# Four products of the second block's mixer in seven quarter products instead of eight, with GpSimd making the weight sums; the gathers' first batches and last search moved

## The reference, cut to what matters

```
def peer_ffn(h, w_q, sub_keys, u, v):
    q = (ht @ w_q).reshape(T, PEER_HEADS, 2, PEER_DKEY // 2)
    s = jnp.einsum('thpc,hpnc->thpn', q, sub_keys)
    v1, i1 = lax.top_k(s[:, :, 0], K)
    v2, i2 = lax.top_k(s[:, :, 1], K)
    ...                      # best 16 of the 256 sums of a head: idx, and g by softmax
    a = jnp.einsum('thkd,td->thk', jnp.take(u, ib, axis=0), xb)
    return jnp.einsum('thk,thkd->td', gelu(a) * gb, jnp.take(v, ib, axis=0))

def token_mixer(h, w_in, w_conv, b_conv, b_igate, b_fgate, ...):
    xin = h @ w_in
    qa, ka, va, qm, km, vm, og, ig, fg = jnp.split(xin, cuts, axis=-1)
    attn = dilated_attention(rms(qa), rms(ka), va)
    qkm = silu(causal_short_conv(concat([qm, km]), w_conv, b_conv))     # 4 taps
    hm = mlstm_chunkwise(heads(qm), heads(km), heads(vm), log_i, log_f)
    hm = sigmoid(og) * rms_norm(hm, mlstm_norm_g)
    return concat([attn, hm]) @ w_out
```

## Time and profile before

| | us |
|---|---|
| three runs, median (range) | 1301.77 (1300.29 to 1303.67) |
| the profiled execution | 1299.79 |
| its span in the trace | 1296.4 |
| PE / DVE / ACT / POOL busy | 1189.7 / 890.4 / 251.0 / 321.2 |
| mean granted TensorE clock, share of full speed | 0.972 |

### The profile page before, as it was taken

How to read it: one execution, slowest core, us unless ns; L and a number is a source line. 1 busy time by engine, 2 the same in 40 slices (tenths; PEclk the granted TensorE clock), 3 DMA queues, 4 the chain that set the end, 5 groups by cost and what they waited for, 6 DMA issues and landing times.

```text
span 1296.4 us, 13569 instructions
## 1 busy us (share of the span) xinstructions
PE 1189.7 (92%) x4848; PEld 727.3 (56%) x4848; DVE 890.4 (69%) x2011; ACT 251.0 (19%) x644; POOL 321.2 (25%) x276
## 2 busy tenths in 40 slices
PE   8999999989998888777899887978999999999998
PEld 7657997664555444333334333333347557999943
DVE  4766865488787767777786775656448876567656
ACT  2133210221111111112211112111211441112100
POOL 0100000145554344354435544544000000000000
PEclk9999999999999999899899999889999999999999
DMA  8441657799999999999999999999657756437441
GB/s 321 169 156 66 246 209 272 282 395 396 421 421 420 422 415 419 418 417 413 415 417 418 421 388 422 421 422 421 227 215 256 215 195 250 173 112 252 183 154 64
DMA packets 92754, 399.23 MB, mean 308 GB/s; under 512 B 6480, under 2 KB 9936, under 8 KB 59792
## 3 DMA queue, kind: packets, MB, share of 16 engines
q0 software_dynamic: 37440, 270.30, 50.6%
q1 hardware_dynamic: 55248, 128.08, 27.9%
HBM read 397.30 MB, written 1.06 MB: 307 GB/s over the span
## 4 chain that ended last, share of the span: by engine, by line
PE 58%; DMA 25%; DVE 12%; ACT 2%; issue 2%; POOL 1%; SPq 0%; DVEq 0%; ACTq 0%
DMA big<-in_peer_uv,idx_t 24%; PE ps L955 12%; PE ps L1265 10%; PE ps L668 10%; PE ps L680 9%; DVE big L2259 5%; PE ps L1329 5%; PE ps L829 2%; PE ps L1193 2%; DMA wring<-in_w_in 1%; PE ps L860 1%; PE ps L728 1%; PE ps L1276 1%; ACT rows L1513 1%; POOL big L1755 1%
## 5 line engine op out<-in xcount | busy, mean ns | idle before, releaser
L955 PE MATMUL ps<-big,rows 128*128 128x512 f32 x1024 | 487.9, 633 | 96.5 <-ACT rows L1513 96.1
L955 PEld LDWEIGHTS ps<-big,rows 128*128 128x128 f32 x1024 | 202.1, 202 | 363.4 <-issue 363.4
L2259 DVE CUSTOM_DVE_ANT_0 big<-big 128x1024 f32<-128x1024 f32 x256 | 307.9, 1225 | 138.1 <-DMA big<-in_peer_uv,idx_t 135.1
L1755 POOL DMA_INDIRECT big<-in_peer_uv,idx_t x256 | 309.9, 1210 | 374.2 <-PE ps L955 312.5
L668 PE MATMUL ps<-wring,big 128*128 128x512 f32 (+1 forms) x304 | 125.9, 571 | 0.0
L1507 ACT ACTIVATE small<-small 128x4 f32<-128x4 f32 (+2 forms) x68 | 13.9, 205 | 511.3 <-DVE small L2264 501.7
L680 PE MATMUL ps<-big,wring 128*128 128x256 f32 x512 | 112.3, 379 | 0.0
L680 PEld LDWEIGHTS ps<-big,wring 128*128 128x128 f32 x512 | 96.6, 190 | 13.2 <-issue 0.5
L668 PEld LDWEIGHTS ps<-wring,big 128*128 128x128 f32 x304 | 57.0, 190 | 62.6 <-issue 61.0
L1513 ACT ACTIVATE rows<-const,small 128x128 f32<-128x128 f32 x256 | 82.2, 390 | 20.4 <-DVE small L2268 19.8
L1265 PE MATMUL ps<-big,wring 128*128 128x128 f32 x576 | 66.7, 275 | 0.9 <-DVE big L2579 0.9
(11 more groups left out here) (340 smaller groups left out, 1228.9 us busy)
## 6 DMA issues: line engine op xcount, KB each, us to landing
wring<-in_w_in SPq DMA_DIRECT2D x16, 2048.0 KB, 8.4
wring<-in_w_ada SPq DMA_DIRECT2D x8, 2048.0 KB, 7.8
wring<-in_w_gate SPq DMA_DIRECT2D x5, 2048.0 KB, 8.1
wring<-in_w_down SPq DMA_DIRECT2D x5, 2048.0 KB, 7.7
big<-in_w_ada SPq DMA_DIRECT2D x4, 2048.0 KB, 10.6
wring<-in_w_up SPq DMA_DIRECT2D x4, 2048.0 KB, 7.9
wring<-in_w_out SPq DMA_DIRECT2D x3, 2048.0 KB, 7.9
wring<-in_peer_wq SPq DMA_DIRECT2D x3, 2048.0 KB, 20.9
```

The costliest lines, as they stand in the source:

```text
L955: last = nc.tensor.matmul(banks[h], diag[:, k % DIAGS, :], v_part[:, ring_at(k), h * 512:(h + 1) * 512], start=False, stop=(k % SLOTS == S ...
L1755: pool.indirect_dma_start(pair_ring[:, ring_at(k), :], None, a["peer_uv"], bass.IndirectOffsetOnAxis(idx_t[:, k:k + 1], 0))\
L2259: nc.vector.tensor_tensor_reduce(u_part[:, ring_at(k), :], u_part[:, ring_at(k), :], h_t[:, b, :], 1.0, 0.0, ALU.mult, ALU.add, a_dot[:, i ...
```

## The change

1. The four products `in2_v`, `in2_qm`, `in2_km`, `in2_vm` are cut into quarters (two token blocks or halves of columns, two halves of the 1024 inputs) and made by seven products P1 to P7 of quarters, as in the feed-forward part. P1, P6, P7 and P4 add up in one PSUM bank ("x"), P5 and P3 in another ("z"), P2 stands alone ("y").
2. DVE makes four sums of the input once (`mix_in`). POOL makes four sums of the weight tile per product (`mix_made`: 128 x 1024 each, the fourth in place in the tile), for each of the four tiles.
3. ACT copies partial results out (`mix_copy`, 128 x 256), DVE adds three pairs per product (`mix_add`, 128 x 256). The convolutions now read their input from SBUF (`conv_in`), since it is a sum of parts.
4. PSUM banks of this stretch are given by hand (`MIX_BANKS`, `LATE_TURN`). ACT's `rsqrt(DA_STAT)` stands behind its copy of P4 of the first product.
5. Gather stage: `kept_query` is cut into 1 + 2 + 1 quarters around batches 1 and 2, `turn_query(1)` goes ahead of batch 0 on PE and `scale(1, 1, gain)` ahead of the dots of batch 0 on DVE; rows 16 to 19 go to places 1 to 4 and rows 20 and 21 to places 8 and 9; the last search starts after batch 43 instead of 42.

```diff
-    starts = {(0, 1): 2, (0, 2): 8, (0, 3): 14, (1, 0): 20, (1, 1): 26, (1, 2): 34, (1, 3): 42}
+    starts = {(0, 1): 2, (0, 2): 8, (0, 3): 14, (1, 0): 20, (1, 1): 26, (1, 2): 34, (1, 3): 43}
...
-    place = [1, 2, 3, 4, 5, 6, 7, 0] * 2 + [8, 9]
+    place = [1, 2, 3, 4, 5, 6, 7, 0] * 2 + [1, 2, 3, 4, 8, 9]
...
             query("peer_q1", 0)
+            turn_query(1)
             experts(0, banks)
-            turn_query(1)
             score(0, 1)
+            wait_turned("n2T", [1])
+            reserved("peer_q1", 1)
+            kept_query(range(0, 1))
             experts(1, banks)
-            wait_turned("n2T", [1])
+            kept_query(range(1, 3))
+            experts(2, banks)
             begin("peer_q1", 1)
-            kept_query(range(4)).then_inc(product_done, 1)
-            experts(2, banks)
+            kept_query(range(3, 4)).then_inc(product_done, 1)
...
-            by_rows("in2_v", hT2, blocks=[0])
+            mix(0, "P1")
+            mix(0, "P2")
             wait_turned("n4T", [1])
             by_rows("in2_q", hT2, blocks=[1])
             by_rows("in2_k", hT2, blocks=[1])
-            by_rows("in2_v", hT2, blocks=[1])
-            for n in ("in2_qm", "in2_km"):
-                by_cols(n, src=hT2)
+            for t, product in MIX_ORDER[2:MIX_ORDER.index((3, "P1"))]:
+                mix(t, product)
...
+            def mix_made(t):
+                q, n = [[mix_quarter(t, f, k) for k in range(2)] for f in range(2)], TILE_NO[MIX_TILES[t]]
+                add = nc.gpsimd.tensor_tensor
+                pool.wait_ge(tile_landed[n % W_SLOTS], 16 * (n // W_SLOTS + 1))
+                if t:
+                    wait_step(pool, t - 1, "P5")
+                add(mix_sums(0), q[1][0], q[1][1], ALU.add).then_inc(mix_summed, 1)
...
+                add(mix_sums(1), mix_sums(0), q[0][0], ALU.subtract).then_inc(mix_summed, 1)
...
+                add(mix_sums(2), q[0][1], mix_sums(1), ALU.subtract).then_inc(mix_summed, 1)
+                add(q[1][0], q[0][0], q[1][0], ALU.subtract).then_inc(mix_summed, 1)
...
+            for t in range(4):
+                mix_made(t)
             pool.wait_ge(ada_made, ADA_ORDER.index(9) + 1)
             gate_row(0)
...
             for m in range(HALF_BATCHES):
                 dots(m)
                 if m == 0:
-                    scale(1, 1, gain)
                     best_keys(0, 0, 1)
...
-                    wait_product(dve, n, h)
+                    if h:
+                        wait_copied(dve, i + 1, "P4")
+                        wait_added(dve, i + 1, "P7")
+                    else:
+                        wait_added(dve, i + 1, "P2")
                     for c2 in range(2):
                         ch = 4 * i + 2 * h + c2
-                        z = bank((n, h), S, c2 * S)
+                        z = conv_in[i + 1][:, (2 * h + c2) * S:(2 * h + c2 + 1) * S]
```

More of the change, by code:

```diff
@@ L206, in product_list @@
     p += half("n3T", 1) + [("ple0", 1), ("ple1", 1), ("in2_q", 0), ("in2_k", 0)] + half("n4T", 1)
[L207 to L209 removed]
+    p += [("mix_y", 0), ("in2_q", 1), ("in2_k", 1), ("mix_z", 0, 0), ("mix_x", 0, 0)]
+    for t in (1, 2):
+        p += [("mix_z", t, 0), ("mix_z", t, 1), ("mix_y", t), ("mix_x", t, 0), ("mix_x", t, 1)]
+    p += [("d_qT", b) for b in range(NB)] + [("d_kT", b) for b in range(NB)] + [("if_parts",), ("mix_y", 3), ("in2_if",)]
+    p += [("d_S", 0, i, g) for i in range(2) for g in range(2)] + [("mix_z", 3, 0), ("m_cols",), ("m_M", 0), ("m_M", 1)]
+    p += [("mix_x", 3, 0)]
     p += [("d_S", 1, i, g) for i in range(2) for g in range(2)] + [("m_S", h) for h in range(GH)] + [("in2_og", 0)]
@@ L1088, in _ @@
             last.then_inc(product_done, 1)
-            by_rows("in2_vm", hT2, blocks=[0])
+            mix(3, "P1")
+            mix(3, "P2")
+            mix(3, "P5")
             wait_moved(pe, "if_parts")
@@ L1106, in scored @@
                         last.then_inc(product_done, 1)
+            mix(3, "P6")
             scored(0)
-            by_rows("in2_vm", hT2, blocks=[1])
+            mix(3, "P3")
+            mix(3, "P7")
             pe.wait_ge(m_rows, 1)
@@ L1123, in _ @@
                 last.then_inc(product_done, 1)
+            mix(3, "P4")
             scored(1)
@@ L1134, in _ @@
             for b in range(NB):
-                wait_moved(pe, "in2_vm", b)
+                wait_added(pe, 3, "P7")
+                wait_copied(pe, 3, "P4")
                 def pair(s_b, h):
@@ L1597, in _, with mix_copy @@
             rms(3, 1)
-            move(va[:, 0, :], "in2_v", 0)
+            def mix_copy(t, product):
+                if product == "P4":
+                    wait_chain(act, t, "x")
+                    to = mix_out(t, 1, 0)
+                else:
+                    if product == "P1" and t >= 2:
+                        act.wait_ge(mix_added, 3 * (t - 1))
+                    wait_step(act, t, product)
+                    to = mix_part(t, ("P1", "P5", "P6", "P7").index(product))
+                nc.scalar.activation(to, mix_bank(t, "z" if product == "P5" else "x"), ACT.Copy).then_inc(mix_copied, 1)
+                if product == "P4":
+                    wait_copied(act, t, "P4")
+                    for n in range(1 + int(MIX_COLS[t])):
+                        act.sem_inc(emptied("mix_x", t, n), 1)
+            for t, product in MIX_COPIES[:MIX_COPIES.index((0, "P4")) + 1]:
+                mix_copy(t, product)
             rsqrt(DA_STAT)
@@ L1601, in _ @@
             exp_and_tanh()
-            move(va[:, 1, :], "in2_v", 1)
+            for t, product in MIX_COPIES[MIX_COPIES.index((0, "P4")) + 1:MIX_COPIES.index((3, "P1"))]:
+                mix_copy(t, product)
             for c in range(2):
@@ L2274, in _ @@
             out_added(1, 1)
+            scale(1, 1, gain)
             for m in range(HALF_BATCHES):
```

181 lines of the change are left out of this document (166 added, 15 removed).

## The result

The changed kernel is slower: 1318.78 us, median of four runs (1317.56 to 1320.62), against 1301.03 (1300.12 to 1303.67) for the kernel before; the ratio is 1.0133, 95% interval 1.0121 to 1.0145, so 17.7 us. Its profiled execution took 1318.88 us with a span of 1316.6. That lies in the predicted range of 1295 to 1320, near its upper end, 4.8 us above the 1314 predicted.

What follows compares the result with a forecast made beforehand. PE was taken as busiest, with DVE only 2.7 us ahead and then full in the mixer, and DMA pacing the gathers. Sum: 1299.8 - 1.5 - 2.2 + 16.2 = 1312.3 profiled, 1314 as median; 8-in-10 range 1295 to 1320.

Steps and rivals of the forecast that it cites:

- What bounds the kernel: Mixer stage: DVE 2.7 us ahead of PE at the row chain, then full, so further PE gains become waits.
- POOL's sums, the deciding term: Mixer stage: POOL's sixteen additions and DVE's SBUF instructions block each other in turns; m_rows 15.8 us late; chance 0.55.
- The wait of 8 us before the fourth product: Mixer stage: in2_vm is loaded 11 us late, so PE idles about 8 us ahead of its product.
- +16.2 at the end of the stage: End of the mixer stage: net lateness with full blocking, after 1.0 of additions less 0.6 of slack; bounds -1.9 and +16.2.
- the 12 to 17 us named as a sign: Mixer stage: being longer by this much was to show the blocking forecast right.
- PE alone 6.0 us: Mixer products: seven quarter products in place of eight save PE 3.3 us by rows and 2.7 by columns.
- the mixer 1.9 faster with no hold-up: Mixer stage: if POOL blocks nobody, 1.9 of PE's 6.0 us come through, as DVE is full.
- the rival at 1296: Mixer stage: a POOL read does not hold DVE up; 5.6 us gained in all; chance 0.25.
- The convolution from SBUF: DVE's convolutions: three taps fall from 1.52 to 1.26 us, 0.4 saved per channel, 3.2 in all, bounds 0 and 4.
- Banks cost nothing: PSUM banks: those reused first wait for DVE steps ahead of the data anyway; without that cover, up to 1 us.
- First batches 1.5: Gather stage, batches 0 to 2: gather 17 issued 1.9 us sooner; gain 1.5 us, bounds 0 and 1.85.
- Last search 2.2: Gather stage, 750 to 765 us: starting one batch later removes a DMA dip; gain 2.2 us, bounds 0 and 2.6.

Runs made afterwards that it cites:

- e2: Changed kernel with each of POOL's sixteen weight sums made for only 4 of its 1024 columns: 1300.06 us, ratio 1.0007 to the kernel before.
- e6: As e2, with the second token block's score banks chosen like those of the kernel before: 1298.65 us, ratio 0.9989.
- e8: Changed kernel with all four modulation sums of ada8 ahead of the first convolution, so in2_vm can load sooner: 1318.82 us, ratio 1.0147.
- e12: Kernel before, products and convolutions untouched, plus sixteen unused 128x1024 GpSimd additions of constants: 1306.24 us, ratio 1.0053.
- e11: Kernel before with only the last search moved to after batch 43 instead of 42: ratio 1.0005.
- e9: Kernel before with only the gather part of the change, the same kernel as e4 measured again: 1298.26 us, ratio 0.9987.
- e4: Kernel before with only the gather part of the change: 1298.25 us, ratio 0.9984.

## Why the prediction was right, and where not

- *What bounds the kernel.* Right: DVE was 2.7 us ahead of PE at the row chain and then full. Most of what PE gained became waits (e2, e6).
- *POOL's sums, the deciding term.* Right in kind and nearly in size. Predicted: norms end at 987.5, `ada8` used up at 1008.8, `in2_vm` 11 us late, the row chain 15.8 late. Measured: 988.1; the load at 1009.45, 11.6 late; the row chain's end at 1040.1, where before it was 1022.99: 17.1 late, 16.0 against a stage that begins 1.1 us later. What the one row at 1012.89 showed for POOL held for both engines. That the size fits so well is luck in part. The turns at the third and fourth tile were put at 17.4 to 18.4 us and took 15.0 (1.5, 1.5, 4.1, 1.9 and 6.0 in the rows above); but the convolutions, which were to be 3.2 us shorter, were 1.0 shorter. The two misses nearly cancel.
- *The wait of 8 us before the fourth product.* 4.98 us there, and 5.73 us before `in2_if`, which the prediction didn't have: ACT's copy of the gate columns stands behind DVE's convolutions. The first is no cause (e8); the second was still there in e8, and by its row it is DVE's backlog once more.
- *"+16.2 at the end of the stage."* The term was mis-sized: 19.2, outside the 12 to 17 us named as a sign. It is right up to `m_cols` (16.3). Behind it are 2.85 us more than before. The quarter P4, 1.9 us, stands there now; before, no part of this product stood behind `m_cols`. The scores took 0.8 us longer, at a lower clock.
- *PE alone 6.0 us, the mixer 1.9 faster with no hold-up; the rival at 1296.* Wrong. e2 is that case: its stage is 2.9 us longer than before and not 1.9 shorter, and its time is by its ratio 0.9 us above the kernel before and not 5.6 below. Of these 6.5 us the banks make up to 3.7 and the gather stage 1.8; of the mixer's 1.9 us about one is there. The convolution from SBUF was to save 3.2 us (taps of 0.42): it saved 0.13 a channel, 1.0 in all, since three taps take 1.52 us from SBUF as from PSUM. The 0.42 was a TENSOR_TENSOR's; these taps are of another form, with a column of scalars, each waiting for the one before. And it is this move that opened the 32 instructions of DVE's convolutions to GpSimd: beside its additions the taps passed in e12, where they read PSUM.
- *Banks cost nothing.* Wrong where DVE isn't late: 1.5 to 3.7 us in e2. The step that failed is "the ones reused first wait for DVE steps that come ahead of the data anyway": the bank of `m_cols` waits for ACT.
- *First batches 1.5.* Borne out, though never run alone: the seventeenth gather goes 1.1 to 1.7 us sooner than in the kernel before and e12, and the whole gather part is 1.4 to 2.4 us faster in two comparisons, with nothing from the last search.
- *Last search 2.2.* Wrong: nothing measurable (e11). The dip went as foreseen, but a dip's missing bytes are no measure of the gain, when they are missing again 30 us later.
- *The sum.* It was 1312.3 for a profiled 1318.9. The end of the stage makes 3.0 of the 6.6, the gather stage 2.3 (1.4 gained for 3.7), the first gather's later issue in this one execution 2.5, and the time outside the span gives 1.1 back (2.3 us against 3.4).

## What to carry to other kernels

GpSimd is no free adder beside a full VectorE: nearly every VectorE form measured here whose tensors all lie in SBUF (TENSOR_REDUCE and MEMSET are the exceptions) waits for the whole GpSimd addition under way, however small it is itself. So give GpSimd such additions only where VectorE is idle or reads PSUM, and cut them into short instructions. Moving a VectorE operand from PSUM to SBUF is not neutral even if its duration stays: it ends that immunity. Before counting a saving on the busiest engine, follow it to the next point where it meets the second busiest: here, of 6 us of fewer matmuls about one came through, without any hold-up by GpSimd.

## What the runs showed of the hardware

- GpSimd's one-operand multiplication by 1.0 of 128x1024 takes longer than its addition of two operands (40 in 110.8 us, 2.77 each, against 2.36), and holds VectorE far less: beside it four two-operand additions of 256 columns took 2.27 us (1.43 alone), and four SCALAR_TENSOR_TENSOR 1.66 (1.68 alone). One execution showed this.
- GpSimd's memsets left VectorE's two-operand forms alone (1.43 for four), but not the one-operand forms, against what was expected: with constants 3.45 us for four, where 0.90 is its own time, and with a column of scalars 4.21, where 1.38 is. ScalarE's copies held nothing.
- TENSOR_REDUCE was not held: 1.22 us for 1024 columns from SBUF beside GpSimd's additions in the changed kernel and in e12, where VectorE's additions around it were. VectorE's MEMSET was not held either: 1.09 us for four beside the additions as alone.
- The granted clock can fall without idle time ahead. In e9 it was 0.84 and 0.81 from 1025 to 1035 with TensorE busy throughout, and sixteen score records took 3.57 us; in e4, the same kernel, it was 1.00 and they took 2.10. TensorE's rows ahead of it are the same in both profiles.
